# A hybrid attention step: the prompt in two halves of attention and MLP, with the key selection hosted by other stages

## Reference

```python
score = jnp.where(adm[None], sum_over_heads(relu(qi . ki) * wi), -jnp.inf)
_, sel = lax.top_k(score, k_top)                       # 256 keys per query
logits = qa . k_sel / 8 - slope_a * dist;  o_a = softmax(logits) @ v_sel      # 8 heads
p = softmax(qb . kb / 8 - slope_b * dist); o_b = (p[:, :, 0] - lam * p[:, :, 1]) @ vb   # 4 heads
h = h + concat(o_a, rmsnorm(o_b)) @ w_o
h = h + relu(rmsnorm(h) @ w_up) ** 2 @ w_down
y = rmsnorm(h)
```

## Time and profile before

| | us |
|---|---|
| median of 3 runs | 4193.75 |
| lowest and highest | 4191.43, 4200.74 |
| the profiled execution | 4200.52 |
| its span | 4199.0 |
| keys, queries and the sample's start | 0 to 720 |
| sample attention after that | 720 to 975 |
| prompt attention | 975 to 2404 |
| MLP with the output projection | 2404 to 4199 |

### The profile page before, as it was taken

How to read it: one execution, slowest core, us unless ns; L and a number is a source line. 1 busy time by engine, 2 the same in 40 slices (tenths; PEclk the granted TensorE clock), 3 DMA queues, 4 the chain that set the end, 5 groups by cost and what they waited for, 6 DMA issues and landing times. The chain is left out here.

```text
span 4199.0 us, 51724 instructions
## 1 busy us (share of the span) xinstructions
PE 3644.4 (87%) x18889; PEld 3054.7 (73%) x18889; DVE 2370.8 (56%) x4401; ACT 1594.9 (38%) x2386; POOL 186.5 (4%) x373
## 2 busy tenths in 40 slices
PE   8989996883777777778787789999999999989997
PEld 6867882443676766778776668887888788879996
DVE  4335651443778888888887444445445444544334
ACT  2123431122465665667664432332323232322221
POOL 0001110000000000000000010001000100010000
PEclk9999995995588988899898899999999999999999
DMA  5556435617222111111110142333223322322121
GB/s 155 155 156 207 160 123 167 202 66 209 61 45 52 42 43 33 43 26 35 26 26 16 35 147 80 103 107 130 96 104 110 110 100 100 124 97 76 64 80 45
DMA packets 279855, 394.21 MB, mean 94 GB/s; under 512 B 29584, under 2 KB 181136, under 8 KB 270864
## 3 DMA queue, kind: packets, MB, share of 16 engines
q1 hardware_dynamic: 244208, 336.77, 25.7%
q0 software_dynamic: 12160, 44.18, 3.3%
q10 hardware_dynamic: 23328, 11.22, 1.2%
HBM read 320.32 MB, written 71.80 MB: 93 GB/s over the span
## 5 line engine op out<-in xcount | busy, mean ns | idle before, releaser
L1135 PE MATMUL pPV<-pV,pPTr 128*128 128x64 f32 (+1 forms) x3648 | 544.0, 298 | 48.5 <-ACT pPTr L1208 41.3
L1135 PEld LDWEIGHTS pPV<-pV,pPTr 128*128 128x128 f32 x3648 | 523.0, 216 | 75.9 <-issue 57.0
L2033 PE MATMUL fUP<-fA_hi,fW_hi 128*128 128x512 f32 (+1 forms) x1280 | 419.4, 360 | 19.5 <-DVE fA_lo L2205 19.5
L2163 ACT ACTIVATE fRU<-fUP 128x512 f32<-128x512 f32 (+1 forms) x128 | 80.0, 625 | 931.3 <-PE fUP L2033 931.3
L2033 PE MATMUL fDN<-fW_hi,fU_hi 128*128 128x512 f32 x1088 | 423.7, 389 | 2.2 <-DVE fY L2303 2.2
L2033 PE MATMUL fDN<-fW_lo,fU_hi 128*128 128x512 f32 x1088 | 423.4, 389 | 0.0
L2033 PE MATMUL fDN<-fW_hi,fU_lo 128*128 128x512 f32 x1088 | 423.3, 389 | 0.0
L2033 PE MATMUL fUP<-fA_lo,fW_hi 128*128 128x512 f32 (+1 forms) x1280 | 418.5, 359 | 0.0
L2033 PE MATMUL fUP<-fA_hi,fW_lo 128*128 128x512 f32 (+1 forms) x1280 | 417.9, 359 | 0.0
L2199 DVE TENSOR_TENSOR fW_lo<-fW_raw,fW_hi 128x2048 fp32r<-128x2048 f32 x144 | 333.4, 2337 | 132.3 <-ACT fW_hi L2118 132.3
L1183 ACT ACTIVATE pX<-pX,pmx 128x144 f32<-128x144 f32 (+15 forms) x256 | 310.4, 1212 | 194.1 <-DVE pmx L1280 193.8
(11 more groups left out here) (234 smaller groups left out, 6320.3 us busy)
## 6 DMA issues: line engine op xcount, KB each, us to landing
fW_raw<-w_up SPq DMA_DIRECT2D x64, 1024.0 KB, 5.1
fW_raw<-w_down SPq DMA_DIRECT2D x64, 1024.0 KB, 4.9
qT<-qOUT SPq DMA_DIRECT2D x40, 512.0 KB, 3.0
sKB<-cache_kb SPq DMA_DIRECT2D x8, 2048.0 KB, 13.7
sVB<-cache_vb SPq DMA_DIRECT2D x8, 2048.0 KB, 8.3
pQA<-qT SPq DMA_DIRECT2D x64, 256.0 KB, 5.0
pQB<-qT SPq DMA_DIRECT2D x64, 256.0 KB, 5.1
fW_raw<-w_o SPq DMA_DIRECT2D x16, 1024.0 KB, 5.5
```

Of the source, the lines that this page charges most:

```text
L1135: mm = pe.matmul(pv[:, 0:size], PTr[n % 3][:, j - 4 * k, :], V[:, j, a:a + size], start=(j == 0), stop=(j == blk[t] - 1))
L2033: mm = pe.matmul(o, stationary[a], m[b], start=first and i == 0, stop=last and i == 2)
```

## The change

`attend_prompt` and `feed_forward` are each called twice, for tiles 0 to 7 and 8 to 15 (the second MLP also has the sample's tile). `attend_prompt` selects no keys any more: masks come from DRAM. The selection of a tile is a chain of 30 windows (25 halvings and five tail passes, 84 steps), and two chains run in a host stage. In `attend_sample` they are tiles 7, 6, 5, 4 from window 0 on and 3, 2, 1 from window 12, all counts on ScalarE; 4 windows stand beside each stream's relu, 9 beside each differential and 3 beside each sparse job. In the first `feed_forward` they are tiles 8, 10, 12, 14 from window 0 and 9, 11, 13, 15 from window 8; a group has 70 windows, 6 in the output projection and 8 in each slice, and in the UP half the chains take turns between ScalarE and VectorE. A window of VectorE is `pick_small` (one-column steps) and `pick_pass` (a count or tail pass), of ScalarE `pick_signs`; the mask's store and the next tile's load are issued on ScalarE's queue (`pick_hand_over`). In `attend_prompt` POOL loads the mask, multiplies it and adds the distance table, for two tiles in advance. The MLP's loops are unrolled; ScalarE makes both the square and its high part, and U2 is gone.

```diff
-def attend_prompt(nc, kT, kv, qT, scores, bounds, dist, ident, lambdas, sub_g, oT):
+def pick_signs(act, chain, window):
+    at = picking(chain, window)
+    if at is None or at[1] >= HALVINGS or not chain.on_act(window):
+        return
...
+    act.wait_ge(chain.s_pick, i * PICK + count_step(w, 1))
+    act.activation(chain.D[:, 0:n], chain.S[:, 0:n], ACT.Sign, bias=chain.v[:, 2:3] if w else 0.0, scale=-1.0,
+                   accum_out=chain.v[:, 3:4]).then_inc(chain.s_pick, 1)
+def pick_hand_over(engine, chain, window, scores, masks):
...
+    engine.wait_ge(chain.s_pick, (i + 1) * PICK)
+    engine.dma_start(masks[t * P:(t + 1) * P, 0:n], chain.D[:, 0:n]).then_inc(chain.s_store, 16)
+    if i + 1 < len(chain.tiles):
+        pick_load(engine, chain, i + 1, scores)
+def attend_prompt(nc, tag, tiles, kT, kv, qT, masks, dist, ident, lambdas, sub_g, oT):
...
             keys(0)
             queries(QA, 0, 0, H_A, s_qa)
+            for dst, src in ((idn[:, :], ident), (DT[:, :], dist), (lam4, lambdas), (gB[:, :], sub_g)):
+                sp.dma_start(dst, src).then_inc(s_c, 16)
+            for c in range(groups[0]):
+                values(c)
             queries(QB, 0, BBLK, 2 * H_B, s_qb)
+            map_keys(0)
...
+            def add_distance(t):
+                made = t - first_masked
+                pool.wait_ge(s_m[t % 2], 16 * (made // 2 + 1))
+                pool.tensor_scalar(DA[t % 2][:, 0:n_of[t]], DA[t % 2][:, 0:n_of[t]], -BIG, 0.0, ALU.mult, ALU.add)\
+                    .then_inc(s_mb, 1)
+                pool.wait_ge(s_mb, made + 1)
+                pool.tensor_tensor(DA[t % 2][:, 0:n_of[t]], DA[t % 2][:, 0:n_of[t]],
+                                   DT[:, nearest[t]:PKEYS], ALU.add).then_inc(s_da, 1)
...
+            for t in range(TN):
+                inverse_rms(t)
+                if first_masked + 2 <= t + 2 < TN:
+                    load_mask(t + 2)
+                    add_distance(t + 2)
...
-                if m < H_A and t > 0:
-                    dve.wait_ge(s_sel, t * SEL)
+                if m == 0 and picked:
+                    dve.wait_ge(s_da, t - first_masked + 1)
...
-                if t + 1 < PT:
-                    for k in range(*select_steps(m)):
-                        select(t + 1, k)
...
 def attend_sample(...):
+                    if k == 2:
+                        for window in windows[B + g][:3]:
+                            act_window(act, window)
...
                 act.activation(R[b % 2], LG[0:H_I * Q, 0:SKEYS], ACT.Relu).then_inc(s_ir, 1)
+                for window in windows[b]:
+                    act_window(act, window)
...
                     softmax(g + 1)
+                for window in windows[B + g][3:]:
+                    act_window(act, window)
...
             keys(0)
+            for b in range(B):
+                for window in windows[b]:
+                    dve_window(dve, window)
             take(0)
...
-                    for k in range(SEL * g // SPAN, SEL * (g + 1) // SPAN):
+                    steps = range(SEL * g // SPAN, SEL * (g + 1) // SPAN)
+                    mine = windows[B + g]
+                    for j, k in enumerate(steps):
+                        for window in mine[len(mine) * j // len(steps):len(mine) * (j + 1) // len(steps)]:
+                            dve_window(dve, window)
...
 def feed_forward(...):
+        def on_act(c, window):
+            w = window % GW - OW
+            return w < 0 or w % 8 >= 4 or (w + c) % 2 == 0
...
-            with engine.Fori(0, UPS - 1, 1) as k:
+            for k in range(UPS):
                 pair(k)
...
-                        act.wait_ge(s_u2, g * FCS + k * FC + (f + 1 + ONE))
-                        act.activation(U_hi[:, f, 0:nt * P], U2[:, 0:nt * P], ACT.Copy).then_inc(s_uh, 1)
+                        act.wait_ge(s_ru, c + 1)
+                        act.activation(U_hi[:, f, 0:nt * P], RU[:, 0:nt * P], ACT.Square).then_inc(s_uh, 1)
+                        act.wait_ge(s_uh, c + 1)
+                        act.activation(RU[:, 0:nt * P], RU[:, 0:nt * P], ACT.Square).then_inc(s_u2, 1)
...
+                        act_window(act, g * GW + OW + k * 8 + f)
...
                         c = g * FCS + k * FC + f
-                        dve.wait_ge(s_ru, c + 1)
-                        dve.wait_ge(s_ul, c + ONE)
-                        dve.tensor_tensor(U2[:, 0:nt * P], RU[:, 0:nt * P], RU[:, 0:nt * P],
-                                          ALU.mult).then_inc(s_u2, 1)
-                        dve.wait_ge(s_uh, c + 1)
-                        dve.tensor_tensor(U_lo[:, f, 0:nt * P], U2[:, 0:nt * P],
+                        dve_window_small(dve, g * GW + OW + k * 8 + f)
+                        dve.wait_ge(s_u2, c + 1)
+                        dve.tensor_tensor(U_lo[:, f, 0:nt * P], RU[:, 0:nt * P],
                                           U_hi[:, f, 0:nt * P].bitcast(F32), ALU.subtract).then_inc(s_ul, 1)
                         if f < 2:
                             w_lo_part(g, k + 1, 2 + f)
+                        dve_window_pass(dve, g * GW + OW + k * 8 + f)
...
                         dve.tensor_tensor(Y[:, t, cols], DN[o % 4][:, :], Y[:, t, cols], ALU.add)\
                             .then_inc(s_dv, 1)
+                        if h == 1 and t < 4:
+                            dve_window_small(dve, g * GW + OW + k * 8 + 4 + t)
+                            dve_window_pass(dve, g * GW + OW + k * 8 + 4 + t)
...
+EARLY = (([7, 6, 5, 4], 0), ([3, 2, 1], 12))
+LATE = (([8, 10, 12, 14], 0), ([9, 11, 13, 15], 8))
...
-    attend_prompt(nc, kT, kv, qT, scores, bounds, p_dist, ident, lambdas, sub_gain, oT)
-    feed_forward(nc, x, oT, w_o, w_up, w_down, mlp_gain, final_gain, ident, y)
+    attend_prompt(nc, "p", range(0, HALF), kT, kv, qT, masks, p_dist, ident, lambdas, sub_gain, oT)
+    feed_forward(nc, "f", 0, (4, 4), x, oT, w_o, w_up, w_down, mlp_gain, final_gain, ident, y, LATE, scores, masks,
+                 bounds)
+    attend_prompt(nc, "r", range(HALF, PT), kT, kv, qT, masks, p_dist, ident, lambdas, sub_gain, oT)
+    feed_forward(nc, "g", HALF, (4, 5), x, oT, w_o, w_up, w_down, mlp_gain, final_gain, ident, y)
```

More of the change, by code:

```diff
@@ L16 @@
 from contextlib import ExitStack
+from dataclasses import dataclass
 import numpy as np
@@ L855, in select_step, with picking @@
     ins.then_inc(s_sel, 1)
-def attend_prompt(nc, kT, kv, qT, scores, bounds, dist, ident, lambdas, sub_g, oT):
+PICK = 1 + HALVINGS * SEL_EACH + 8
+PICK_WINDOWS = HALVINGS + 5
+@dataclass
+class Chain:
+    tiles: list
+    start: int
+    period: int
+    S: object
+    D: object
+    v: object
+    widths: object
+    on_act: object
+    s_pick: object
+    s_load: object
+    s_store: object
+def picking(chain, window):
+    i, w = divmod(window - chain.start, chain.period)
+    return (i, w) if 0 <= i < len(chain.tiles) and w < PICK_WINDOWS else None
@@ new lines, in pick_pass @@
+def pick_pass(dve, chain, window, powers, bounds):
+    at = picking(chain, window)
+    if at is None:
+        return
+    i, w = at
+    tail = count_step(HALVINGS, 1)
+    if w < HALVINGS:
+        if chain.on_act(window):
+            return
+        if w == 0:
+            dve.wait_ge(chain.s_load, 16 * (i + 1))
+            if i > 0:
+                dve.wait_ge(chain.s_store, 16 * i)
+        steps = [count_step(w, 1)]
+    else:
+        steps = ([tail + 1], [tail + 3], [tail + 4], [tail + 5, tail + 6], [tail + 7])[w - HALVINGS]
+    for k in steps:
+        pick_step(dve, chain, i, k, powers, bounds)
@@ L1697, in _ @@
                     softmax(g + 1)
+                for window in windows[B + g][3:]:
+                    act_window(act, window)
+            for chain in chains:
+                for window in range(windows[-1].stop, chain.start + len(chain.tiles) * PERIOD):
+                    pick_hand_over(act, chain, window, scores, masks)
             for k in range(2):
@@ L1701, in _ @@
                                ACT.Copy).then_inc(s_fc, 1)
+            for chain in chains:
+                act.wait_ge(chain.s_store, 16 * len(chain.tiles))
         @block.vector
@@ L2191, in _ @@
             groups(act, group)
+            for chain in chains:
+                for window in range(len(sizes) * GW, chain.start + len(chain.tiles) * PERIOD):
+                    pick_hand_over(act, chain, window, scores, masks)
+                act.wait_ge(chain.s_store, 16 * len(chain.tiles))
         @block.vector
```

372 lines of the change are left out of this document (226 added, 146 removed).

## The result

The changed kernel takes **4090.27 us** (median of 4 runs, 4078.45 to 4093.63); the kernel before 4195.76 us beside it. The ratio is 0.9743, 95% interval 0.972 to 0.9766: 2.6% faster, where I had forecast 4217 us and "slower" with a chance of 0.56. The profiled execution took 4088.69 us, its span is 4086.9 us, 112.1 less than before.

What follows compares the result with a forecast made beforehand. The prediction took the attention to be bound by TensorE waiting for VectorE, held up by key selection. Its terms, -235 + 125 + 70 + 55 + 8 = +23 on 4193.75 us, gave 4217 us, range 4105 to 4310.

Steps and rivals of the forecast that it cites:

- The attention: Prompt attention without selection: TensorE's waits for VectorE's takes and combines go, -235 us, ends -173 and -320.
- The check that I set beside it: Prompt attention: fifteen selection tails on VectorE, scaled by columns from the longest, 21.2 us, make 180 us.
- Rival A: Prompt attention: the clock comes back to a mean of 0.90, matmuls 83 us shorter, 4134 us; chance 0.17.
- The sample: Sample attention hosting the selection of tiles 1 to 7: a loss of +125 us, ends +85 and +185.
- The split: One attention and MLP stage becomes two, with standstill and second start: +70 us, ends +55 and +95.
- The MLP: First MLP hosting the selection of tiles 8 to 15: a largely covered loss, +55 us, ends +15 and +110.
- Rival B: First MLP covers its guests: Y additions seldom late, the 55 us goes, 4162 us; chance 0.15.
- POOL: Prompt attention: POOL adding distances, 76 us of its work, disturbs VectorE by +8 us, 0 to +58.
- Rival D: Prompt attention: POOL's passes hold VectorE up, +58 instead of +8 us, 4267 us; chance 0.10.
- Edits that I had at nothing: MLP: unrolling the loops and losing the U2 buffer, 0 us, since TensorE runs UP and DN back to back.

Runs made afterwards that it cites:

- w3: The changed kernel with the 25 halvings and the nine tail steps of the selection both run again in its attentions, result unused: 4428.79 us.
- w1: The changed kernel with only the nine tail steps of the selection run again on VectorE in its two attentions, result unused: 4232.65 us.
- w2: The changed kernel with only the 25 halvings, counts on ScalarE included, run again in its two attentions, result unused: 4290.26 us.
- c2: The kernel before, with extra matmuls for TensorE's waits in the attention (up to nine per tail, three ahead of each combined pair), nothing removed: 4204.24 us.
- h1: The changed kernel without any prompt key selection: no stage hosts chains, and the attentions read keys in place of masks: 3919.86 us.
- h3: The changed kernel without the chains in the first MLP (selection of tiles 8 to 15 left out, keys read as those masks): 4038.48 us.
- h2: As h1, without prompt key selection, but the prompt again in one attention and one MLP: 3861.84 us.

## Why the prediction was wrong

*The attention: here it failed.* The step was "What is removed from the path is bounded by the two waits: 173.3 alone below, 173.3 + 71.1 = 244.4 with all combine waits", and the value -235. The stage fell by 345.7, because the sum left TensorE's 1069 busy microseconds as they were, and they fell by 112.8. That idle time fell by 232.9 us, so close to the 235, is luck: the two waits gave only 244.4 - 76.6 = 167.8 of it, and most of the rest came from waits that my sum does not have, above all those for ScalarE's copies of the transposes, before and in the two parts after:

```profile
PE pPV L1135 <- ACT pPTr L1208: 41.3, 40, 2.3
```

```profile
PE pPV L1245 <- ACT pPTr L1310: 11.5, 35, 0.4
...
PE rPV L1245 <- ACT rPTr L1310: 0.3, 1, 0.3
```

The number that should have stopped me stood in the earlier trace rows, a granted clock of 0.83. A matmul at a low clock between two waits is counted as work and not as a wait, so the row of waits holds only part of what the selection's steps cost. A better bound from the same rows was the stage with TensorE at the clock of a stage with few waits, an estimate: 1071.66 x 0.83 / 0.98 = 908 us of matmuls, measured 956, and the waits that stay. w3 shows it by the way back: the selection's steps alone brought 215 us of idle time and 123 us of slower matmuls. The check that I set beside it, 180 us for fifteen tails, could not warn me, since it priced tails alone; w1 gives 139 for them and w2 196 for the halvings, for which my 235 left 55.

*Rival A was the right case, undersized.* I gave it a chance of 0.17, a clock of 0.90 and 83 us; measured were 0.93 and 0.97 and 113 us. Of what I held against it, the pairs did keep waits: 40.5 of the 71.1 us before combined maps stayed, but none is over 1.4 us where the longest was 9.1, and the clock came back all the same. Whether the clock is a cause by itself, or only falls with the pace of the takes, stays open: w1 to w3 show that the selection's steps bring both waits and slow matmuls, and c2 could not part the two. The Trainium skill, "TensorE: Matmul & The Clock Gate", section "HAM oscillation — how this bites in real kernels", describes TensorE falling to the low clock when waits keep cutting its work, and the matmuls after a wait paying for it. The traces agree on the fall: 0.84 with the selection between takes, 0.93 and 0.97 without.

*The sample: right in its sum.* +125 forecast, 126.4 in the stage, 119 by h1 and h3. The parts missed and their errors cancel, which is luck: eight differential rounds grew by 81 us (I said 92), the sparse ones with the sample's end by 39 (I said 20), the score stage by 6.5 (I said 13).

*The split: near.* +70 forecast, 72.8 outside the attentions by h1 and h2, 58 in all. The gap of 43 us is 42.5 in the trace.

*The MLP: right in its sum, not in its parts.* +55 forecast, 52 by h3, of which 21 are Y's waits (22.6 against 1.6 in h3). I had 45 for those, growing with the columns; they do not grow from the first group to the second, 11.3 us in each. The other waits of TensorE there grew by 10 us and its matmuls by 18 (818.6 busy instead of 801.0, clock 0.96 against 0.97). Rival B falls.

*POOL: nothing.* Takes with the tables that POOL makes (rDA, the sparse jobs, beside which POOL makes the next tile's table) and takes with the fixed table (rDT) in the second attention, groups by line and shape:

```profile
L1372 DVE CUSTOM_DVE_ANT_0 rX<-rLG,rDA 128x1024 f32<-128x1024 f32 x64 | 78.3, 1223 | 158.0 <-PE rTP L1234 154.6 <-PE rLG L1213 3.3
L1372 DVE CUSTOM_DVE_ANT_0 rX<-rLG,rDT 128x1024 f32<-128x1024 f32 x64 | 78.2, 1221 | 123.8 <-PE rTP L1234 123.8
```

The sparse takes last 1.223 us in the mean, the others 1.221, and the longest of each 1.226 and 1.227. A take that lies within POOL's passes, which run in tile 14 from 2894.66 to 2901.26, is as short as the rest:

```profile
2897.23 1.23 DVE L1372 CUSTOM_DVE_ANT_0 rX<-rLG,rDA 128x1024 f32<-128x1024 f32 x1 [3.85 <-PE rTP L1234]
```

Rival D falls. The Trainium skill, "SBUF — State Buffer", section "Who interferes with whom", says that an instruction of VectorE with at most one operand in SBUF, outside the two-port modes, does not contend with GpSimd. The trace agrees for the takes, by the numbers above; the subtraction of the earlier trace rows, with two operands in SBUF, was a case of the other kind.

*Edits that I had at nothing: no gain shown.* The MLP in one part, unrolled and without U2, takes 1796.1 us in h2 where the kernel before takes 1806.5 (from the first UP of a group to that of the next 408.1 and 408.4 us, before 411.2 and 413.0). That is no proof of a gain: in c2, whose MLP is that of the kernel before, it takes 1798.2 us, and its groups 409.8 and 409.6.

With the terms as measured the sum is -346 + 126 + 73 + 47 = -100, where the spans differ by 112; 10 of the 12 us between them are this difference of the MLP. The forecast fell with one term, and its sign with it.

## What to carry to other kernels

Before pricing the removal of work from an engine that another one waits for, look at the granted clock of that stage, and bound the gain by what the waiting engine needs at the clock it has elsewhere, not by its waits. Here a third of the gain, 113 of 346 us, lay in matmuls that ran slowly between waits. What the clock is worth without taking the other engine's work away, no run here shows. Guest work was cheapest where all the engines that it needs already stood still: the same windows cost 4 to 9 us less in a round when four of them were moved into the wait for logits.

## What the runs showed that I had not expected

The nine tail steps cost 0.87 us of the stage for each microsecond of VectorE's time, the 25 halvings 0.50, and with about as much idle time of TensorE (107 us against 118) the halvings made its matmuls 89 us longer, the tails 21. That many short delays do more to the clock than one long one in each tile is a reading: the halvings are also more work, on two engines. And one column block more changed a pair from 11.2 to 15.7 us; from tile 13 to 14, one block as well, it was 10.6 to 11.2. What differs in tile 15 is the third pass, of 16 columns, through two PSUM halves; a tile of that size without it was not run.
